# Head outputs turned to features by VectorE and a way through DRAM instead of by TensorE

## What is computed

```python
# first block, one layer: 8 mLSTM heads (values of 256) and 16 delta-net heads of 128
h = x + sum_over_kinds(gate * (gated_norm(heads(x)) @ w_out))       # out of 2 x 2048 features
# second block, two layers
y = concat([band_attention * silu(a_z),      # 8 heads of 128
            gated_linear_attention * silu(b_z),
            memory_attention * silu(m_z)])   # 4 heads of 128, 256 memory rows
x = layer_norm(ALPHA * x + y @ w_out)
```

## Time and profile before

| | |
|---|---|
| median of 3 runs | 2156.32 us (2155.24 to 2160.36) |
| the profiled execution | 2158.48 us |
| its span | 2156.8 us, TensorE's granted clock 0.996 |
| PE / DVE / ACT / POOL busy | 99% / 60% / 51% / 6% |
| DMA | 400.51 MB, mean 186 GB/s |

### The profile page before, as it was taken

How to read it: one execution, slowest core, us unless ns; L and a number is a source line. 1 busy time by engine, 2 the same in 40 slices (tenths; PEclk the granted TensorE clock), 3 DMA queues, 4 the chain that set the end, 5 groups by cost and what they waited for, 6 DMA issues and landing times.

```text
span 2156.8 us, 30821 instructions
## 1 busy us (share of the span) xinstructions
PE 2135.6 (99%) x11444; PEld 1765.4 (82%) x11444; DVE 1284.8 (60%) x1589; ACT 1107.6 (51%) x1472; POOL 138.2 (6%) x215
## 2 busy tenths in 40 slices
PE   9999999999999999999999999999999999999998
PEld 7888888888888777788878888888888788888886
DVE  6455546464544867676766565566545845566466
ACT  6554545454444748474755454445444544445343
POOL 7000000000000100001010000000000210000002
PEclk9999999999999999999999999999999999999999
DMA  9866565666565555454646765745558566555644
GB/s 340 261 182 194 173 194 179 184 197 203 181 202 175 156 163 151 142 166 134 182 140 216 255 187 169 203 147 168 174 178 290 171 200 180 158 159 165 195 160 154
DMA packets 208218, 400.51 MB, mean 186 GB/s; under 512 B 13296, under 2 KB 30209, under 8 KB 207710
## 3 DMA queue, kind: packets, MB, share of 16 engines
q1 hardware_dynamic: 199440, 369.94, 55.3%
q0 software_dynamic: 6352, 20.49, 3.1%
q10 hardware_dynamic: 2304, 8.39, 1.2%
HBM read 389.94 MB, written 8.82 MB: 185 GB/s over the span
## 4 chain that ended last, share of the span: by engine, by line
PE 90%; ACT 3%; DVE 3%; issue 3%; DMA 1%; DVEq 0%; ACTq 0%; SPq 0%
PE stream_psum L646 27%; PE stream_psum L648 26%; PE stream_psum L647 26%; PE heads_psum L616 2%; ACT w_high L1087 1%; DVE work L1671 1%; DVE w_low L1508 1%; ACT work L1087 1%; PE heads_psum L1004 1%; PE heads_psum L966 1%; PE heads_psum L947 1%; PE heads_psum L838 1%; DMA w_raw<-in_w_in 1%; DMA w_raw<-in_w_mem_kv 1%; PE heads_psum L819 1%
## 5 line engine op out<-in xcount | busy, mean ns | idle before, releaser
L1508 DVE TENSOR_TENSOR w_low<-w_raw,w_high 128x1024 fp32r<-128x1024 f32 x688 | 831.2, 1226 | 638.1 <-ACT w_high L1087 636.8
L1087 ACT ACTIVATE w_high<-w_raw 128x1024 fp32r<-128x1024 f32 x688 | 712.5, 1058 | 467.6 <-PE stream_psum L648 404.6
L646 PE MATMUL stream_psum<-w_high,x_high 128*128 128x512 f32 x1856 | 740.0, 399 | 1.6 <-issue 1.1
L648 PE MATMUL stream_psum<-w_high,x_low 128*128 128x512 f32 x1856 | 723.7, 390 | 0.0
L647 PE MATMUL stream_psum<-w_low,x_high 128*128 128x512 f32 x1856 | 723.1, 390 | 0.0
L646 PEld LDWEIGHTS stream_psum<-w_high,x_high 128*128 128x128 f32 x1856 | 348.7, 188 | 74.8 <-issue 3.5
L648 PEld LDWEIGHTS stream_psum<-w_high,x_low 128*128 128x128 f32 x1856 | 348.4, 188 | 73.3
L647 PEld LDWEIGHTS stream_psum<-w_low,x_high 128*128 128x128 f32 x1856 | 348.8, 188 | 69.9 <-issue 1.9
L646 PE MATMUL stream_psum<-w_high,y_high 128*128 128x512 f32 x896 | 353.9, 395 | 2.8 <-DVE y_low L1945 2.8
L647 PE MATMUL stream_psum<-w_low,y_high 128*128 128x512 f32 x896 | 350.0, 391 | 0.0
L648 PE MATMUL stream_psum<-w_high,y_low 128*128 128x512 f32 x896 | 350.0, 391 | 0.0
(11 more groups left out here) (318 smaller groups left out, 1235.8 us busy)
## 6 DMA issues: line engine op xcount, KB each, us to landing
w_raw<-in_w_in SPq DMA_DIRECT2D x528, 512.0 KB, 4.5
w_raw<-in_w_out SPq DMA_DIRECT2D x128, 512.0 KB, 5.1
w_raw<-in_w_mem_kv SPq DMA_DIRECT2D x32, 512.0 KB, 5.7
work<-rows_scratch POOLq DMA_DIRECT2D x8, 512.0 KB, 4.8
proj<-in_mem_t SPq DMA_DIRECT2D x8, 256.0 KB, 6.7
work<-in_x_t SPq DMA_DIRECT2D x4, 512.0 KB, 6.8
residual<-in_x SPq DMA_DIRECT2D x2, 1024.0 KB, 9.8
mkv_scratch<-proj POOLq DMA_DIRECT2D x4, 512.0 KB, 4.1
```

The source lines that it names most:

```text
L646: pe.matmul(acc, hi[:, k, sl(m)], w, start=first, stop=False)
L648: return pe.matmul(acc, lo[:, k, sl(m)], w, start=False, stop=final)
L1087: return act.activation(dst, src, func, **kw)
L1508: tt(WL[:, c % RING, :], RAW[:, c % RING, :], WH[:, c % RING, :].bitcast(F32), ALU.subtract).then_inc(lo_done, 1)
```

## The change

In the ten groups of the kinds `ml` and `attend` the outputs are no longer turned by TensorE. VectorE turns 32x32 blocks (`turn`, two instructions), placing the result so that partition 32a+f of a row holds part a of the tokens' features; POOL stores it into a DRAM scratch of 128x1024 in four DMAs (one per 32 partitions, runs of 256 floats) and loads it back in one (`across`), after which features stand on the partitions. ScalarE waits for that load and makes the high part from SBUF, VectorE the low part. The steps `out0` and `out1` of TensorE are gone, the copies stand further down (14 steps after the turn, for `attend` 13 for VectorE), and for `ml` VectorE's residue is cut in two instructions per tile. The `dn` and `gla` groups stay as they were.

```diff
+    turned_d = nc.dram_tensor("turned_scratch", (P, U), F32, kind="Internal").ap()
...
+        def by_features(u):
+
+            return wk(u).rearrange("p (a c m t) -> p c m a t", a=4, c=4, m=M)
...
+            def across(n, at, to):
+
+                for a in range(4):
+                    pool.dma_start(bass.AP(turned_d.tensor, a * S, [[U, QUART], [QUART * U, 4], [1, S]]),
+                                   wk(at)[sl(a, QUART), :].rearrange("p (c r) -> p c r", c=4)).then_inc(turned_out, 16)
+                wait_alone(pool, turned_out, n * 64 + 64)
+                pool.dma_start(wk(to), turned_d).then_inc(turned_in, 16)
...
             with pool.Fori(1, 4) as g:
                 wait_alone(pool, *done(ML_V, "arg", g - 1))
                 ml_rows(g)
+                wait_alone(pool, *done(ML_V, "turned", g - 1))
+                across(g - 1, 9, 10)
+            pool.wait_ge(*done(ML_V, "turned", 3))
+            across(3, 9, 10)
...
                 pool.wait_ge(rel_st, l * 16 + 16)
+                pool.wait_ge(*done(AT_V["m"], "turned", l))
+                across(4 + 3 * l, 8, 7)
                 wait_alone(pool, out_lo, NCH + (l * 16 + 36))
...
+                for i in range(2):
+                    pool.wait_ge(*done(AT_V["a"], "turned", 2 * l + i))
+                    across(5 + 3 * l + i, 8, 7)
...
# TensorE, ml
-                yield from gap(8)
-                yield from outputs(ML_PE, done(ML_V, "fg", g), F.rearrange("p (m n) -> p m n", m=M), 0)
+                yield
# TensorE, attend
-                yield from gap(3)
-                yield from outputs(steps, done(dve, "fg", n), wk(7).rearrange("p (m n) -> p m n", m=M), 2)
+                yield
...
# ScalarE
+            def outputs_in(n, kt, col, u, to=YH):
+
+                wait_alone(act, turned_in, n * 16 + 16)
+                for j in range(4):
+                    kw = {} if col is None else {"scale": NC_[:, bass.ds(col(j), 1)]}
+                    f(to[:, bass.ds(kt + j, 1), :].rearrange("p k (m a t) -> p (k m) a t", m=M, a=4), by_features(u)[:, j], ACT.Copy, **kw).then_inc(out_hi, 1)
+                yield
# ScalarE, ml
-                yield from gap(3)
-                yield from outputs(ML_PE, g, g, g * 4, lambda j: g * 4 + (16 + j), 0)
+                yield from gap(14)
+                yield from outputs_in(g, g * 4, lambda j: g * 4 + (16 + j), 10)
# ScalarE, attend
-                yield from gap(5)
-                yield from outputs(steps, n, q, kt, None, 2, OUTPUTS[(q - 8) // 4][0])
+                yield from gap(16)
+                l, i = divmod(q - 8, 4)
+                yield from outputs_in(4 + 3 * l + max(0, i - 1), kt, None, 7, OUTPUTS[l][0])
...
# VectorE
+            def turn(F, T):
+
+                for m in range(M):
+                    last = dve.transpose(wk(T).rearrange("p (c n m t) -> p m n c t", c=4, n=4, m=M)[:, m],
+                                         wk(F).rearrange("p (m n c t) -> p m n c t", m=M, n=4, c=4)[:, m])
+                return last
+
+            def outputs_in(q, kt, col, u, to=(YH, YL)):
+
+                for j in range(4):
+                    dve.wait_ge(out_hi, NCH + (4 * q + (2 * (j // 2) + 2)))
+                    yh, yl = [t[:, bass.ds(kt + j, 1), :].rearrange("p k (m a t) -> p (k m) a t", m=M, a=4) for t in to]
+                    if col is None:
+                        tt(yl, by_features(u)[:, j], yh.bitcast(F32), ALU.subtract).then_inc(out_lo, 1)
+                        continue
+                    for m in range(M):
+                        last = stt(yl[:, m], by_features(u)[:, j, m], NC_[:, bass.ds(col(j), 1)], yh[:, m].bitcast(F32), ALU.mult, ALU.subtract)
+                    last.then_inc(out_lo, 1)
                 yield
# VectorE, ml
-                yield from gap(2)
-                yield from outputs(ML_PE, g, g, g * 4, lambda j: g * 4 + (16 + j), 0)
+                yield
+                dve.wait_ge(*done(ML_V, "fg", g))
+                turn(10, 9).then_inc(*signal(ML_V, "turned"))
+                yield from gap(14)
+                yield from outputs_in(g, g * 4, lambda j: g * 4 + (16 + j), 10)
# VectorE, attend
-                yield from gap(2)
-                yield from outputs(steps, n, q, kt, None, 2, OUTPUTS[(q - 8) // 4])
+                yield
+                dve.wait_ge(*done(AT_V[kind], "fg", n))
+                turn(7, 8).then_inc(*signal(AT_V[kind], "turned"))
+                yield from gap(13)
+                yield from outputs_in(q, kt, None, 7, OUTPUTS[(q - 8) // 4])
```

More of the change, by code:

```diff
@@ L165, in build @@
         memt_out, memt_in = sem("mem_features_stored"), sem("mem_features_loaded")
+        turned_out, turned_in = sem("turned_stored"), sem("turned_loaded")
         rows_out, rows_in, kv_in = sem("rows_stored"), sem("rows_loaded"), sem("kv_loaded")
@@ L177, in build @@
                                        "rs1", "rs2", "kd", "rt", "scan", "negm", "ems", "neb", "hb"])
-        ML_PE = steps_of(sem("ml_pe"), ["q", "k", "scores", "pv", "out0", "out1"])
+        ML_PE = steps_of(sem("ml_pe"), ["q", "k", "scores", "pv"])
         ML_ACT = steps_of(sem("ml_act"), ["to", "tz", "q", "k", "expw", "sq", "root"])
-        ML_V = steps_of(sem("ml_dve"), ["arg", "g1", "g2", "mask", "p", "den0", "den", "rden", "h", "ss", "rs", "fr", "fg"])
+        ML_V = steps_of(sem("ml_dve"), ["arg", "g1", "g2", "mask", "p", "den0", "den", "rden", "h", "ss", "rs", "fr", "fg", "turned"])
         LVS = range(3, 6)
@@ L199, in build @@
         DN_PL = steps_of(sem("dn_pool"), ["maskg"] + [f"zero{i}" for i in range(4)] + ["upper8", "halves8", "u8", "ut3", "ut4"])
-        AT_PE = {k: steps_of(sem(f"{k}_pe"), ["k", "q", "scores", "pt", "pv", "out0", "out1"]) for k in "am"}
+        AT_PE = {k: steps_of(sem(f"{k}_pe"), ["k", "q", "scores", "pt", "pv"]) for k in "am"}
         AT_ACT = {k: steps_of(sem(f"{k}_act"), ["tz", "q", "exp", "pt"]) for k in "am"}
-        AT_V = {k: steps_of(sem(f"{k}_dve"), ["k", "g"] + (["bias"] if k == "a" else []) + ["max0", "max1", "neg", "pt", "rs", "f", "fg"]) for k in "am"}
+        AT_V = {k: steps_of(sem(f"{k}_dve"), ["k", "g"] + (["bias"] if k == "a" else []) + ["max0", "max1", "neg", "pt", "rs", "f", "fg", "turned"]) for k in "am"}
         GL_PE = steps_of(sem("gla_pe"), ["q", "k", "logit", "b", "d"] + [f"l{l}" for l in range(1, 9)] + ["pv", "out0", "out1"])
@@ L754, in ml @@
                 yield from gap(3)
-                q, k, w, F = wk(0, 512), wk(0.5, 512), wk(2, 768), wk(10)
+                q, k, w = wk(0, 512), wk(0.5, 512), wk(2, 768)
                 pe.wait_ge(*done(ML_ACT, "k", g))
```

## The result

| | before | after |
|---|---|---|
| median of the runs compared (4 each) | 2157.16 us (2155.24 to 2160.36) | 2144.34 us (2143.74 to 2146.69) |
| profiled execution | 2158.48 us | 2146.69 us |
| its span | 2156.8 us | 2145.0 us |

The ratio is 0.9942, 95% interval 0.9929 to 0.9954: faster by 12.8 us in the medians (the interval is 9.9 to 15.3 us), by 11.8 in the spans. The sign was right, the size was not: 8.3 us were worked out, which lies outside the interval.

What follows compares the result with a forecast made beforehand. TensorE, busy 99% of the span, was taken as the bound, its instruction order being the time. -9.1 (transpositions) + 0.5 (DMA traffic) + 0.3 (end) = -8.3 us, giving 2148.0 us from a median of 2156.3, range 2145.5 to 2150.5.

Steps and rivals of the forecast that it cites:

- TensorE, removed: Ten groups each lose 8 transpositions on TensorE, 0.91 us per group: -9.1 us.
- They start without a wait, so there is no wait to give back: At TensorE's 8 transpositions per group: removing them returns their own 0.91 us, with no wait in play.
- POOL's queue: Bias loads behind the memory group's stores come some 16 us later but are needed only 100 us on: cost 0.
- DMA traffic, +0.5: 10 MB more on 400, crowded in layer 0's second attention group: +0.5 us, bounds 0 and 3.6.
- the end, +0.3: Last normalization's subtraction (2.29 us) moves later on VectorE and pushes its tail: +0.3 us, bounds 0 and 0.6.
- VectorE: hidden: VectorE's added 1.5 us of transpositions per group, +1.7 us of residues in mLSTM groups, hidden by its lead: cost 0.
- The way: Through DRAM, POOL's four stores and one load: 13.6 us, between 9.0 and 20.0; fits the room, cost 0.
- the mLSTM room: Time from the turn's end until data must be there for ScalarE's copies in mLSTM groups: 15.1 us.
- The attention room of 16.3 us: Time from the turn's end until the data must be there in attention groups: 16.3 us, middle value fits by 2.7.
- rival B: The way outlasts its room and ScalarE stands before its copies; at 18.0 us, 2170 us, slower; chance 0.10.
- The base: Starting time for the sum: median of the runs, 2156.3 us, 2.2 below the profiled execution's 2158.5.
- The range: Forecast's own range for the whole kernel: 2145.5 (way free, nothing at the end, scatter of a microsecond) to 2150.5 us.

Runs made afterwards that it cites:

- the idle transpositions: Changed kernel with TensorE again transposing a constant tile eight times at each of the ten old places, read by nobody: 2157.3 us against 2157.32 before, ratio 1.0.

## Why the forecast was too high

**TensorE, removed: right.** 9.1 us forecast. The trace gives 0.895 in each mLSTM group and 0.90 in each of layer 0, some 9.0 for ten, and the idle transpositions cost 9.0 when put back. Busy time fell by 9.3.

**"They start without a wait, so there is no wait to give back": this step failed.** It was true of the eight instructions, and I took it for true of TensorE's whole program. Removing 80 instructions moved all later ones, and 2.2 us in the delta-net groups vanished (4.1 against the kernel that differs in the transpositions only); the two places near 765 to 771 and 887 us gave 1.2 and 1.5 us, less 0.4 lost elsewhere in the stretch. Their three entries, 2.5 us of issue, were in the list of waits that I had read as one number, "some 15 us together". Shown: the stalls come with instructions elsewhere in TensorE's program (back with the transpositions, in all ten groups or four; back with warm-up matmuls) and are not tied to data, since the products and what they wait for are the same. It does not follow that fewer instructions stall less: the changed kernel has an issue wait of 1.6 us at chunk 16 that the kernel before has not (0.8 in its second trace, 0.6 and 2.4 with 14 and 16 warm-ups, at most 0.3 from 20 on). That this one has the same cause is not shown. How much such stalls give back or take was luck for this forecast. Not shown: what runs short at these places. That it is the supply of instructions would fit bursts of 32 to 64 small products broken after the same count, but no view here records that supply, and the counts 14 to 28 gave no rule. It stays open.

**POOL's queue, "Cost 0": it cost nothing, and may have given 0.75 us.** I had noted that the bias loads would come some 16 us later (in layer 0 they came some 14 us later: 1361.42 for 1352.95, with TensorE 5 us ahead) and asked only whether that was too late. It is also away from where they held up the weights that TensorE was about to need. Of the 1.1 us less in layer 1 beyond the transpositions, 0.75 is that stall, present in two of the four traces with early loads, and 0.4 is scatter.

**DMA traffic, +0.5, and the end, +0.3: both measured nothing.** Layer 0, with the crowded second attention group, gave 0.90 per group in full. After the last stream matmul (-11.63) the span still ends 11.8 earlier; the end lost nothing.

**VectorE: hidden, as forecast.** The transposition took 686 ns, at the lower bound (0.68), not 0.75; two overlap to 1.30 us per group. The residues in halves took 343 ns each, 2.18 us for eight where four took 1.66: +0.5, not +1.7. ScalarE's copies from SBUF take 1.71 us for 1.57.

**The way: right.** 12.2 to 15.1 us, forecast 13.6 between 9.0 and 20.0. The first mLSTM copies began 0.7 us ahead of their limit, and the run with the copies earlier met the mLSTM room within 0.5 us. The attention room of 16.3 us was too small by about one: with the idle transpositions the way of the second attention group of layer 0 took 16.9 us, 17.2 from the end of the turn, and TensorE waited for no residue. The rule of the Trainium skill, page "VectorE: DVE Perf Modes" (section "Rules for kernel authors"), to leave 128x128 transpositions to TensorE where PSUM will do, does not hold here: TensorE's eight cost 0.9 us of the engine that sets the time, the other way costs none of it. (The factor of 19 that the prediction names is that page's, against the chip's own transposing DMA and for a large innermost stride; no run here shows it.) And its price when the room is short is more than the one for one of rival B, as the clock showed.

**The base.** The sum stood against a median of 2156.3; in the four runs compared it is 2157.2, which hides another 0.9 us of the gain. In all: forecast gain 8.3; plus 0.8 not charged, 2.2 delta-net, 1.1 layer 1, less 0.7 for a slower first stretch in this execution (48.3 to 51.0 in the traces with 12 warm-ups; the issue wait of 1.6 us is in it) and 0.1 for the term itself, is 11.6, against 11.63 at the last stream matmul.

The range failed for the same reason: with nothing charged the sum is 2147.2, and its lower end, 2145.5, allows for scatter alone below that (1.7 us, where the text names one). It had no place for stalls given back, though the list of waits had 2.5 us of "issue" and 0.5 us of a late residue in it.

## What to carry to other kernels

Where one engine is busy 99% of the time, work moved off it is worth its length on that engine, however much longer the other way is, so long as the room is worked out from the first instruction queued behind its wait; check that room by making it too small on purpose. When instructions are removed from a full engine, every small wait in its list is in play, the unexplained ones too: carry them into the range as a possible gain, when instructions are added as a loss, and allow for a new one either way. A transfer that moves later should be asked both who misses it and whom it no longer disturbs.

## What was not expected of the hardware

- A burst of 32x32 matmuls, or the matmul behind it, can stand for 0.3 to 1.4 us, waiting for nothing that the profile shows, at places that mostly repeat between executions and change with the instructions ahead; the delta-net stretch is 460.5 to 464.8 us over fourteen traces, 460.5 and 460.8 with one order of TensorE's instructions, 463.0 to 463.8 with another.
- A wait of TensorE of 5.0 us was followed by 5.3 us at a granted clock of 0.50, so it cost 7.4 us and not 5. The waits of 2.9 us in the attention groups were followed by matmuls at that pace too.
- The 32x32 transposition of 128x512 floats takes 686 ns, as long as an elementwise operation of that size (682 ns).
